# Block-border convolution taps on GpSimd, reordered low parts, and a third seven-product block in eleven groups

## The reference, cut to what matters

```python
def conv_glu_ffn(h, w_gate, w_up, conv_w, conv_b, w_down):   # h 256x2048, w_gate and w_up 2048x8192
    g = h @ w_gate
    u = h @ w_up
    gp = jnp.pad(g, ((0, 0), (CONV_WIDTH - 1, 0), (0, 0)))
    g = conv_b + gp[:, 0:S] * conv_w[0]
    for j in range(1, CONV_WIDTH):                            # CONV_WIDTH = 3
        g = g + gp[:, j:j + S] * conv_w[j]
    return (jax.nn.gelu(g, approximate=True) * u) @ w_down    # w_down 8192x2048
```

## Time and profile before

| | |
|---|---|
| median of three runs | 1418.74 us |
| the profiled execution | 1419.19 us, its span 1417.4 us |
| PE busy | 1406.1 us, 99% |
| DVE busy | 1235.0 us, 87% |
| ACT busy | 822.2 us, 58% |
| POOL busy | 358.5 us, 25% |
| granted TensorE clock | 0.999 |
| groups 0 to 14 | about 442 to 1074 us of the span, 42.16 us each |

### The profile page before, as it was taken

One profiled execution on the slowest core, in us unless ns is written; L12 is line 12 of the kernel. 1 busy time (PEld: TensorE's weight loads), 2 busy tenths in 40 slices (PEclk: granted clock), 3 DMA queues, 4 the chain that ended last, 5 costly groups with the idle time before them and its releaser, 6 DMA issues.

```text
span 1417.4 us, 18897 instructions
## 1 busy us (share of the span) xinstructions
PE 1406.1 (99%) x6502; PEld 1172.3 (83%) x6502; DVE 1235.0 (87%) x1867; ACT 822.2 (58%) x1082; POOL 358.5 (25%) x609
## 2 busy tenths in 40 slices
PE   9999999999999999999999999999999999999997
PEld 9888888888878888888888888888888888888886
DVE  6867778975587899989999999999998999999996
ACT  7455544554475656655655655556656666666663
POOL 0702020620003234443324444234444000000000
PEclk9999999999999999999999999999999999999999
DMA  8765656555557677767677776677777576666662
GB/s 265 223 182 158 193 183 192 164 164 178 178 165 242 198 228 238 237 208 228 213 219 240 234 228 208 219 227 224 231 231 240 177 236 212 209 198 210 202 214 93
DMA packets 149706, 293.75 MB, mean 207 GB/s; under 512 B 17232, under 2 KB 30832, under 8 KB 149360
## 3 DMA queue, kind: packets, MB, share of 16 engines
q1 hardware_dynamic: 132416, 274.71, 61.6%
q0 software_dynamic: 16384, 16.81, 4.3%
q10 hardware_dynamic: 816, 1.09, 0.2%
HBM read 273.67 MB, written 2.10 MB: 195 GB/s over the span
## 4 chain that ended last, share of the span: by engine, by line
PE 93%; DVE 4%; DMA 1%; ACT 1%; issue 0%; SPq 0%; POOL 0%; DVEq 0%; ACTq 0%
PE psum L2115 48%; PE psum L1888 7%; PE psum L1892 7%; PE psum L1890 7%; PE psum L2096 5%; PE psum L2098 5%; PE psum L2097 5%; PE psum L1855 3%; DVE w_lo L1595 2%; PE psum L1859 2%; DMA stage<-in_w_qkv 1%; PE psum L1936 0%; DVE up_T L1606 0%; PE psum L1942 0%; ACT w_hi L927 0%
## 5 line engine op out<-in xcount | busy, mean ns | idle before, releaser
L2115 PE MATMUL psum<-w_hi,hT 128*128 128x512 f32 x1696 | 463.4, 389 | 0.0
L2115 PEld LDWEIGHTS psum<-w_hi,hT 128*128 128x128 f32 x1696 | 318.3, 188 | 66.2 <-issue 0.2
L2115 PE MATMUL psum<-w_lo,hT 128*128 128x512 f32 x848 | 261.1, 389 | 0.0
L1125 DVE TENSOR_TENSOR w_lo<-stage,w_hi 128x1024 fp32r<-128x1024 f32 x141 | 175.5, 1250 | 90.0 <-ACT w_hi L657 88.6
L657 ACT CAST w_hi<-stage 128x1024 fp32r<-128x1024 f32 x141 | 147.8, 1051 | 179.3 <-PE psum L1892 142.5
L1595 DVE TENSOR_TENSOR w_lo<-stage,w_hi 128x1024 fp32r<-128x1024 f32 (+1 forms) x198 | 219.4, 1136 | 11.4 <-ACT w_hi L927 11.4
L1097 POOL DMA_DIRECT2D gate_rows_f<-gate_T x256 | 134.8, 536 | 368.4 <-DVE gate_T L1472 315.6
L927 ACT CAST w_hi<-stage 128x1024 fp32r<-128x1024 f32 (+1 forms) x198 | 190.1, 984 | 57.0 <-PE psum L2115 42.0
L2115 PEld LDWEIGHTS psum<-w_lo,hT 128*128 128x128 f32 x848 | 159.2, 188 | 33.0
L1097 POOL DMA_DIRECT2D up_rows_f<-up_T x256 | 134.6, 534 | 45.4 <-DVE up_T L1472 36.0
L1888 PE MATMUL psum<-w_hi,hT 128*128 128x512 f32 x312 | 124.9, 400 | 0.0
(11 more groups left out here) (256 smaller groups left out, 2584.4 us busy)
## 6 DMA issues: line engine op xcount, KB each, us to landing
stage<-in_w_qkv SPq DMA_DIRECT2D x93, 512.0 KB, 3.7
stage<-in_w_gate SPq DMA_DIRECT2D x88, 512.0 KB, 4.2
stage<-in_w_up SPq DMA_DIRECT2D x88, 512.0 KB, 5.2
stage<-in_w_down SPq DMA_DIRECT2D x84, 512.0 KB, 4.7
stage_wide<-in_w_down SPq DMA_DIRECT2D x42, 512.0 KB, 4.5
stage_early<-in_w_gate SPq DMA_DIRECT2D x40, 512.0 KB, 4.2
stage_early<-in_w_up SPq DMA_DIRECT2D x40, 512.0 KB, 5.2
stage<-in_w_o SPq DMA_DIRECT2D x32, 512.0 KB, 3.9
```

The costliest lines, as they stand in the source:

```text
L1125: nc.vector.tensor_tensor(w_lo[s][:, :], stage[s][:, :], w_hi[s][:, :].bitcast(F32), ALU.subtract).then_inc(s_lo, 1)
L2115: ins = nc.tensor.matmul(c_bank(G, t, c), a[:, j, ROWS[t]], w[slot_of[v]][:, COLS[c]], start=(q == 0 and j == 0 and n == 0), stop=False, s ...
```

## The change

Six edits:

1. **Borders on GpSimd.** The narrow instructions of taps 1 and 0 leave DVE. For each piece POOL waits until DVE's eight wide ones are done (`s_conv`), then runs four instructions one after the other: multiply the border columns of tap 1 with their weights into a small tile `edge` (7 blocks x 4 x 1 columns), add it, multiply those of tap 0 (7 x 4 x 2), add them. The last one signals `s_edge`, and the GELU waits for that in place of `s_conv`. POOL's order becomes gate moves, up moves, borders for each piece.
2. **Order in a summed block of a group on DVE**: first weight sum (1 and 3), half low part of unit 0, sum 2, low part of unit 1, sum 4, then the low parts of the sums.
3. **A third summed block**, q = 5, in groups 0 to 10 (`EARLY_GROUPS` = 11). Its row sums `h_sums_early` lie in the region that group 11 writes; three row sums are made in the first piece instead of two, at units 9, 11, 13 instead of 10, 12.
4. **Steps.** In groups 0 to 10 block 5 no longer runs steps 10 and 11: tap 2 and tap 1 are both at n = 12, tap 0 at n = 13 (`CONV_AT_THREE`). In groups 11 to 15 they are at n = 10, 11 and 12.
5. **Joint products** stay at the end of block 7 (`JOINT_AT`), which is now two blocks behind the last summed one.
6. **Staging** after a summed block of a group is refilled only once the third weight sum is done, too.

The diff, cut to its core:

```diff
-F_SUMMED = (2, 4)
+F_SUMMED = (2, 4, 5)
+EARLY_GROUPS, ALWAYS = 11, 2
+THREE_IN = tuple(range(EARLY_GROUPS))
...
-        CONV_AT, GATED_AT, ACT_GELU_AT = (10, 11, 13), 15, 15
+        CONV_AT, CONV_AT_THREE, GATED_AT, ACT_GELU_AT = (10, 11, 12), (12, 12, 13), 15, 15
...
-        SUMS = (F_SUMMED,) * F_GROUPS + SUMMED
+        SUMS = tuple(F_SUMMED if G in THREE_IN else F_SUMMED[:ALWAYS] for G in range(F_GROUPS)) + SUMMED
+        JOINT_AT = tuple(blocks.index((G, CHUNK_UNITS - 1)) if G < F_GROUPS
+                         else blocks.index((G, 0)) + SUMS[G][-1] + 3 for G in range(len(SUMS)))
...
                     sp.wait_ge(s_lo, unit_taken(stage_before[u]))
+                    if is_ffn_summed(stage_before[u] // 2):
+                        sp.wait_ge(s_w_sum, 3 * sums_before(stage_before[u] // 2) + 3)
...
             def ffn_gelu(i):
-                act.wait_ge(s_conv, (i + 1) * (2 * CT))
+                act.wait_ge(s_edge, i + 1)
                 nc.scalar.activation(act_g[:, :, :], act_g[:, :, :], ACT.Gelu_apprx_tanh).then_inc(s_gelu, 1)
...
-            move_gate(0)
-            for i in range(1, F_ITERS):
-                move_up(i - 1)
+            def add_edge(i, w, n):
+                e = edge[:, 0:(BLOCKS - 1) * CT * n].rearrange("p (q f c) -> p q f c", q=BLOCKS - 1, f=CT)
+                taps = conv_c[:, w:w + 1, i * CT:(i + 1) * CT].rearrange("p q (f c) -> p q f c", c=1)
+                chain.link(nc.gpsimd.tensor_tensor(e, gate_F[:, 0:BLOCKS - 1, :, QUADRANT - n:QUADRANT],
+                                                   taps.to_broadcast([P, BLOCKS - 1, CT, n]), ALU.mult))
+                chain.settle()
+                return nc.gpsimd.tensor_tensor(act_F[:, 1:BLOCKS, :, 0:n], act_F[:, 1:BLOCKS, :, 0:n], e, ALU.add)
+
+            def add_edges(i):
+                pool.wait_ge(s_conv, (i + 1) * CT)
+                chain.link(add_edge(i, 1, 1))
+                chain.settle()
+                add_edge(i, 0, 2).then_inc(s_edge, 1)
+
+            for i in range(F_ITERS):
                 move_gate(i)
-            move_up(F_ITERS - 1)
+                move_up(i)
+                if i:
+                    pool.wait_ge(s_edge, i)
+                add_edges(i)
...
                     add_tap(1, j, i, act_F[:, :, j, 1:QUADRANT], gate_F[:, :, j, 0:QUADRANT - 1], s_conv_1)
-                    add_tap(1, j, i, act_F[:, 1:BLOCKS, j, 0:1], gate_F[:, 0:BLOCKS - 1, j, QUADRANT - 1:QUADRANT],
-                            s_conv_1)
...
                     add_tap(0, j, i, act_F[:, :, j, 2:QUADRANT], gate_F[:, :, j, 0:QUADRANT - 2], s_conv)
-                    add_tap(0, j, i, act_F[:, 1:BLOCKS, j, 0:2], gate_F[:, 0:BLOCKS - 1, j, QUADRANT - 2:QUADRANT],
-                            s_conv)
...
-            def sums_of_weights(g):
+            def sums_and_unit_lows(g):
                 weight_sum_13(g)
+                unit_low(g, 0, CHUNK)
                 weight_sum_2(g)
+                unit_low(g, 1)
                 weight_sum_4(g)
```

More of the change, by code:

```diff
@@ L139, in layer_kernel @@
         post_g = sb("post_g", [P, D])
-        h_sums = nc.alloc_sbuf_tensor_at("h_sums", [P, len(F_SUMMED), 2, 2, SEQ], F32R, offset=post_at)
+        h_sums = nc.alloc_sbuf_tensor_at("h_sums", [P, ALWAYS, 2, 2, SEQ], F32R, offset=post_at)
         ffn_g_at = (nc.sbuf_base + 31) // 32 * 32
@@ L216, in layer_kernel, with h_sums_of @@
             w_lo.append(place(f"w_lo{s}", [P, UNIT], F32R))
+        h_sums_early = place("h_sums_early", [P, 1, 2, 2, SEQ], F32R, at=44 * KIB)
+        def h_sums_of(x):
+            return h_sums[:, x, :, :, :] if x < ALWAYS else h_sums_early[:, x - ALWAYS, :, :, :]
         for s in range(len(EARLY_SLOTS)):
@@ L255, in layer_kernel @@
         OPENING, WARM_UP = 3, 8
-        table_warm = sb("table_warm", [P, 1])
+        edge = sb("edge", [P, (BLOCKS - 1) * CT * 2])
+        table_warm = edge[:, 0:1]
         psum = ctx.enter_context(nc.psum_tensor("psum", [P, 8 * CHUNK], F32))
@@ L260, in layer_kernel @@
         Q_BANK, V_BANK, WARM_BANK, S_BANK, O_BANK = 0, 2, 5, 6, 7
-        SUMS_AT = tuple(10 + 2 * x for x in range(len(F_SUMMED)))
+        SUMS_AT = tuple(9 + 2 * x for x in range(len(F_SUMMED)))
         GATE_ADD_AT, UP_ADD_AT, ACT_SCALE_AT, GATE_TURN_AT, UP_TURN_AT = 1, 2, 3, 3, 7
-        CONV_AT, GATED_AT, ACT_GELU_AT = (10, 11, 13), 15, 15
+        CONV_AT, CONV_AT_THREE, GATED_AT, ACT_GELU_AT = (10, 11, 12), (12, 12, 13), 15, 15
         PAIR = 2 * P
@@ L356, in layer_kernel @@
         QUADRANT_MOVES = (P // QUADRANT) ** 2
-        s_conv = sem("conv_ready")
+        s_conv = sem("conv_taps_added")
+        s_edge = sem("conv_block_edges_added")
         s_gelu = sem("gelu_ready")
@@ L503, in quarters, with is_ffn_summed @@
             return pair_stage(g).rearrange("p (b n) -> p b n", b=4)
+        def is_ffn_summed(g):
+            return 0 <= g < D0 and is_summed(g)
         def w_sum_of(g):
@@ L523, in p_bank, with conv_at @@
             return bank[4 * (G % 2) + n]
+        def conv_at(i):
+            return CONV_AT_THREE if i in THREE_IN else CONV_AT
         x_rows = x.rearrange("(t p) d -> p t d", p=P)
@@ L866, in normed_sum_high @@
                 act.wait_ge(s_h_sum, 4 * (x + 1))
-                nc.scalar.copy(h_sums[:, x, 0, :, :], h_sum).then_inc(s_h_sum_hi, 1)
+                nc.scalar.copy(h_sums_of(x)[:, 0, :, :], h_sum).then_inc(s_h_sum_hi, 1)
             def conv_tap_2(i):
@@ L951, in take_first_product @@
                 if G < F_GROUPS:
-                    act.wait_ge(s_conv, (G + 1) * (2 * CT))
+                    act.wait_ge(s_edge, G + 1)
                 nc.scalar.copy(y_of(G, 0, 0), p_bank(G, 0)[:, :]).then_inc(s_p1, 1)
@@ L962, in gating_steps @@
                         scale_rows(i, 1)
-                if n == CONV_AT[0]:
+                if n == conv_at(i)[0]:
                     conv_tap_2(i)
@@ L982, in _ @@
                             gating_steps(G, 2 * q + j)
-                if g - 3 in ENDS:
-                    take_first_product(ENDS.index(g - 3))
+                if g in JOINT_AT:
+                    take_first_product(JOINT_AT.index(g))
                 if g == D0 + PAIRS + 3:
@@ L1511, in gated_rows @@
                 dve.wait_ge(s_gelu, i + 1)
-                if i >= min(RETIRED_AT):
+                if i >= EARLY_GROUPS:
                     dve.wait_ge(s_used, block_used(LASTS[i - 1]))
@@ L1540, in normed_sum_low @@
                 dve.wait_ge(s_h_sum_hi, x + 1)
-                nc.vector.tensor_tensor(h_sums[:, x, 1, :, :], h_sum, h_sums[:, x, 0, :, :].bitcast(F32),
+                nc.vector.tensor_tensor(h_sums_of(x)[:, 1, :, :], h_sum, h_sums_of(x)[:, 0, :, :].bitcast(F32),
                                         ALU.subtract).then_inc(s_h_sum_lo, 1)
@@ L1691, in gating_steps @@
                     turn_up(i)
-                if n == CONV_AT[1]:
+                if n == conv_at(i)[1]:
                     conv_tap_1(i)
-                if n == CONV_AT[2]:
+                if n == conv_at(i)[2]:
                     conv_tap_0(i)
@@ L1713, in _ @@
                         gated_sum_low(g)
+                        unit_low(g, 1)
                     else:
-                        sums_of_weights(g)
-                        unit_low(g, 0, CHUNK)
-                    unit_low(g, 1)
+                        sums_and_unit_lows(g)
                     for n in range(2):
@@ L1726, in _ @@
                             gating_steps(G, 2 * q + j)
-                if g - 3 in ENDS:
-                    joint_products(ENDS.index(g - 3))
+                if g in JOINT_AT:
+                    joint_products(JOINT_AT.index(g))
                 if g == D0 + PAIRS + 2:
@@ L2090, in summed_rows_of @@
                 q = blocks[g][1]
-                return h_sums[:, F_SUMMED.index(q), part, :, :] if g < D0 else (a_hi, a_lo)[part](entry[g] + 1)
+                return h_sums_of(F_SUMMED.index(q))[:, part, :, :] if g < D0 else (a_hi, a_lo)[part](entry[g] + 1)
             def rows_product(o, rows, g, w, cs, j, ts, start):
```

2 lines of the change are left out of this document (1 added, 1 removed).

## The result

The changed kernel takes 1451.59 us (median of four runs, 1450.86 to 1451.77) against 1418.79 us for the kernel before on the same chip: 2.3% slower, ratio 1.023 with an interval of 1.0212 to 1.0248. The forecast was 1446.8 us in a range of 1424 to 1459. The profiled execution has a span of 1449.9 us against 1417.4, so 32.5 us are to be explained.

A forecast was written before the change was run, and what follows sets the result against it. PE bounds the kernel now; DVE would in groups 1 to 10. Group 0's +0.6 and ten rounds of 42.21 + 0.5 + 2.2 = 44.9 instead of 42.16 (+27.5) give +28.1: 1446.8 us, range 1424 to 1459.

The forecast's parts named there:

- The bound: Groups 1 to 10: DVE's slack of 2.38 us is gone, it replaces PE as bound, and each added wait counts in full.
- floor of 42.21 us: DVE's round in groups 1 to 10 from instructions alone: 39.78 + 4.05 - 0.48 - 1.14, 0.73 above PE's 41.48.
- small waits: DVE's waits in a round for casts, a preceding low part and tap 2 on ACT: together 0.5 us, bounds 0.1 and 0.8.
- Group 0: DVE's work after the up turn at 455.14 lets PE start group 1 at 484.5 instead of 483.9, +0.6 us.
- The new wait: DVE waits before `gated_rows` for POOL's borders and the GELU: 2.2 us a group, bounds 0.4 and 2.95.
- a wait of 2.6: Alternative: DVE keeps the port lock through both low parts, POOL starts all four instructions after low part 15; wait some 2.6 us.
- Groups 11 to 14: DVE saves 0.48 + 1.14, waits about 2.1; +0.5 fits its idle time, PE stays bound; if not, 1 us in all.
- POOL passing beside DVE: Rival, chance 0.09: POOL's small additions do not exclude DVE's, new wait 0.4 us; time 1427, or 1423 with small waits of 0.1.
- Long POOL instructions: Rival, chance 0.13: POOL's border instructions cost 0.46 us or more each, wait 2.95; time 1458, or 1467 at 0.73 each.
- The faster case: Rival, chance 0.04: PE keeps the lead with DVE's round at 41.48 and no wait; all 33 matmuls gained, -7.48 us, 1411.3.
- only the floor counts: Rival, chance 0.06: the POOL and GELU loop hides behind low parts, rounds near 42.2; time within 2.8 us of now.
- The signs: Groups 1 to 10: DVE idle about 2 us before `gated_rows`, GELU behind POOL, low parts 14, 15 above 1.22, PE idle some 3.

The follow-up runs named there:

- experiment 5: The changed kernel with the border columns left out on every engine, ScalarE waiting for `s_conv`: 1421.65 us, ratio 1.0016.
- experiment 3: The changed kernel with tap 0 at n = 12 instead of 13 in groups 0 to 10, three low parts before the multiply: 1450.89 us, ratio 1.0219.
- experiment 2: The changed kernel without the third summed block in any group, borders on GpSimd and new order kept: 1424.25 us, ratio 1.0034.
- experiment 6: The kernel before with only the new order of low parts between weight sums, and its staging wait: 1419.25 us, ratio 0.9999.
- experiment 4: The changed kernel with one added wait: VectorE waits for GpSimd's borders directly behind tap 0: 1439.71 us, ratio 1.0145.
- experiment 8: The changed kernel with borders in four VectorE instructions, third block only in groups 0, 2, 4, 6, 8, 10, sum 4 earlier, additions later: 1414.19 us, ratio 0.9964.
- experiment 9: The kernel of experiment 8 with the additions back between low parts n = 1, 2 and 3: 1419.65 us, ratio 1.000.

## Why the prediction was right, and where its sizes were off

- **The bound.** "DVE becomes the bound of groups 1 to 10" held. The floor of 42.21 us was a sum of starts of the trace before, and experiment 5 measured 42.6. The 0.39 between them answer to my 0.5 of small waits: 0.37 in the summed blocks, where I had put 0.31, and nothing for low part 13 behind tap 2, where I had put 0.16.
- **Group 0.** Expected: PE begins group 1 at 484.5. It does.
- **The new wait** was 2.2 in the sum and is 2.39. The mechanism, that POOL and DVE exclude each other, was right, as were POOL's times by extrapolation (0.24 and 0.30 expected, 0.242 to 0.307 measured). The step that failed is who goes first: I let POOL's first two instructions slip in behind low parts 14 and 15, because rows of mixed work showed alternation. In neither of those rows does a second low part follow at once: behind the one at 254.53 DVE reads PSUM, and the one at 287.15 had itself waited 1.48 us for ACT. In an unbroken run of low parts POOL is kept out to the end, 2.22 us behind two and 3.37 behind three (experiment 3). I had named this order as well, with a wait of 2.6; with the 0.11 that the sum itself has for POOL's first instruction behind a low part it is 2.45. The measured 2.39 sits between 2.2 and 2.45, and it is the second order that is true. That the sum came so near with the wrong order is luck: in this kernel the two orders cost nearly the same. The Trainium skill ("SBUF — State Buffer", section "SBUF: two separate sides") says that the loser is blocked for a whole instruction, and does not say who wins the next. The traces agree with the block: POOL's multiply ends 0.1 us after the last low part. With the small waits a round is 45.08 in place of 44.91, which in ten rounds is 1.7 us of the 4.4 by which the sum is short on the span (28.1 against 32.5).
- **Groups 11 to 14.** I let them hide everything, "if not, 1 us in all". The term was mis-sized: it is the other 2.7 us, 1.6 of slow clock at the start of group 11 and the stop of PE at the start of the down projection, less what comes back later. DVE's rounds there are 43.50, 42.33 and 42.35 us and not 42.16. I had not seen that edit 2 takes ACT's lead away; experiments 2 and 6 show the 1.51 us that it costs DVE.
- **The rivals.** POOL passing beside DVE would have been 1423 to 1427: ruled out by experiments 3 and 4. Long POOL instructions, 1458: ruled out by their 0.24 to 0.31 us. The faster case hung on a DVE round of 41.48; even without borders it is 42.6. That only the floor counts needed the loop to take under 1.1 us before the GELU; with DVE idle DVE still waits 1.52 us for it (experiment 4).
- **The signs.** The wait before `gated_rows`, the GELU behind POOL and the missing idle time before the additions came as written. Two signs did not: low parts 14 and 15 are not longer beside POOL (2.35 us for the two, as before the change), which again says that DVE is not held up, and PE idles 1.4 to 2.7 us a group, not 3.

## What to carry to other kernels

When the engine at 99% is relieved at the cost of one at 87%, add up the second one's round from instruction starts before anything else; a share over the span hides that it was full where it mattered. Before moving small work to another engine, follow who waits for its answer: here 1.14 us of work became 2.39 us of waiting, and an early wait beat a late one. And where a helper has room only in every second step, ask whether it can run ahead over the border: here that was the difference between 5 us gained and nothing (experiments 8 and 9).

## What the runs showed of the hardware that I had not expected

**GpSimd behind VectorE.** A 28-column GpSimd multiply needs 0.242 us on its own and 3.37 us behind three low parts of 1.13 us each that follow one another (experiments 3 and 4), while the low parts themselves take no longer than without it.

**TensorE's clock.** After five of the six idle stretches of about 2.65 us that begin groups in the changed kernel, the next matmuls ran at half speed for a while, 0.427 us from start to start in place of 0.227; after those of 1.4 to 1.95 us none did. The slow stretch is 6 to 8 matmuls long; it begins at once in three cases (529.60, 709.92, 935.33) and after five or six matmuls at full speed in two (619.75, 845.17). Four stretches of the changed kernel (window, length, busy us and instructions of PE, PEld, DVE, ACT, POOL, granted clock, DMA share, GB/s):

```profile
842.00:845.00 3.00, 0.54 (x3) 0.12 (x1) 2.96 (x5) 1.98 (x3) 0.00 (x0) 1.00 0.02 8
845.00:850.00 5.00, 4.83 (x14) 3.87 (x15) 5.00 (x8) 2.21 (x4) 0.00 (x0) 0.66 0.54 157
932.00:935.00 3.00, 0.67 (x3) 0.20 (x2) 2.93 (x4) 2.14 (x3) 0.00 (x0) 1.00 0.07 27
935.00:940.00 5.00, 4.67 (x14) 3.76 (x15) 5.00 (x8) 2.05 (x4) 0.00 (x0) 0.66 0.46 150
```

The granted clock is 0.66 on the mean of the five us behind the idle time, a mix of the levels 1.2 and 2.4 GHz. While DVE is the bound this costs nothing, since PE waits later anyway; at the start of group 11, where PE takes the lead again, it is 8 x 0.2 = 1.6 us. Why one of the six such stretches (at 800.09) was followed by full clock stays open; no run was made for it.
